# Gated heads over three gate groups, y chunk 7 last, half-width weights split early, x reloaded in portions: one layer of a hybrid encoder trunk on one core

## The reference

```
proj = h @ w_in              # ..., hog/gz (output gates of heads), gate_a, gate_b
o = rmsnorm(o_head, w) * silu(gate of the head)       # 4 HGRN2 heads, 4 delta heads
y_a = o_hg @ w_pa ;  y_b = o_gdn @ w_pb               # 512 -> 1024 each
y = sigmoid(gate_a) * y_a + sigmoid(gate_b) * y_b
x = x + g1 * (y @ w_out)
h = rmsnorm(x, norm_ffn) * (1 + sc2) + sh2
x = x + g2 * ((silu(h @ w_gate) * (h @ w_up)) @ w_down)
return rmsnorm(x, final_norm), new states
```

## Time and profile before

| | us |
|---|---|
| median of three runs | 1112.09 |
| the three runs | 1110.04, 1112.09, 3748.86 |
| the profiled execution, its own time | 1107.67 |
| its span, first to last instruction | 1105.1 |
| TensorE busy in the span | 1048.9 (95%) |
| VectorE, ScalarE busy | 486.3 (44%), 371.2 (34%) |
| mean granted TensorE clock | 0.983 |

### The profile page before, as it was taken

The page is one execution under the profiler, slowest core; times in us unless marked ns, Lnnn a source line. Parts: engine busy times, 40 slices in busy tenths (PEclk is TensorE's granted clock), DMA queues, the critical chain, the costliest instruction groups (busy, mean ns, idle before and its releaser), DMA issues.

```text
span 1105.1 us, 20527 instructions
## 1 busy us (share of the span) xinstructions
PE 1048.9 (95%) x8763; PEld 1009.7 (91%) x8763; DVE 486.3 (44%) x802; ACT 371.2 (34%) x635; POOL 58.0 (5%) x52
## 2 busy tenths in 40 slices
PE   6998999999999999998999997999999999999995
PEld 5887888889999999997999997999999999999995
DVE  3678535272224644735543366433323333233342
ACT  6665343513432234136223213322222222222122
POOL 0002220032201000000000000000000000000000
PEclk9999999999999999999999998999999999999997
DMA  9722222230323253332342322223233232222212
GB/s 328 223 58 58 58 77 58 59 110 21 96 77 112 77 136 108 98 94 78 123 131 70 113 77 77 72 81 95 76 95 88 82 90 82 86 87 89 80 43 81
DMA packets 181253, 103.42 MB, mean 94 GB/s; under 512 B 4498, under 2 KB 179032, under 8 KB 181180
## 3 DMA queue, kind: packets, MB, share of 16 engines
q1 hardware_dynamic: 179340, 96.28, 30.5%
q0 software_dynamic: 1216, 3.84, 1.0%
q10 hardware_dynamic: 624, 2.23, 0.6%
HBM read 99.02 MB, written 3.31 MB: 93 GB/s over the span
## 4 chain that ended last, share of the span: by engine, by line
PE 85%; DVE 6%; ACT 5%; issue 2%; DMA 1%; ACTq 0%; DVEq 0%
PE G L1584 67%; PE R L1590 14%; PE R L1593 2%; DVE cy L1510 1%; PE G L1624 1%; DVE w_lo L1164 1%; DMA raw<-in_w_in 1%; ACT w_hi L874 1%; ACT rn L902 1%; ACT sq L939 0%; ACT Um L911 0%; DVE relT L1341 0%; DMA xtok<-in_x_prompt 0%; ACT L851 0%; DVE val L1525 0%
## 5 line engine op out<-in xcount | busy, mean ns | idle before, releaser
L1584 PE MATMUL G<-h_hi,w_hi 128*128 128x272 f32 x1456 | 427.5, 294 | 10.4 <-DVE w_lo L1164 5.9
L1584 PE MATMUL G<-h_hi,w_lo 128*128 128x272 f32 x1456 | 423.0, 291 | 0.0
L1584 PE MATMUL G<-h_lo,w_hi 128*128 128x272 f32 x1456 | 420.7, 289 | 0.0
L1584 PEld LDWEIGHTS G<-h_hi,w_hi 128*128 128x128 f32 x1456 | 276.0, 190 | 13.1 <-issue 11.5
L1164 DVE TENSOR_TENSOR w_lo<-raw,w_hi 128x1024 fp32r<-128x1024 f32 (+2 forms) x139 | 166.6, 1199 | 261.5 <-ACT w_hi L874 261.0
L1584 PEld LDWEIGHTS G<-h_lo,w_hi 128*128 128x128 f32 x1456 | 276.4, 190 | 0.0
L1584 PEld LDWEIGHTS G<-h_hi,w_lo 128*128 128x128 f32 x1456 | 275.6, 189 | 0.0
L874 ACT ACTIVATE w_hi<-raw 128x1024 fp32r<-128x1024 f32 (+2 forms) x139 | 137.5, 989 | 122.9 <-PE G L1584 108.2
L1584 PE MATMUL G<-a_hi,w_hi 128*128 128x272 f32 x352 | 101.8, 289 | 0.0
L1584 PE MATMUL G<-a_hi,w_lo 128*128 128x272 f32 x352 | 101.7, 289 | 0.0
L1584 PE MATMUL G<-a_lo,w_hi 128*128 128x272 f32 x352 | 101.3, 288 | 0.0
(11 more groups left out here) (233 smaller groups left out, 1321.3 us busy)
## 6 DMA issues: line engine op xcount, KB each, us to landing
raw<-in_w_in SPq DMA_DIRECT2D x48, 512.0 KB, 5.7
raw<-in_w_up SPq DMA_DIRECT2D x44, 512.0 KB, 3.8
raw<-in_w_ada SPq DMA_DIRECT2D x32, 512.0 KB, 4.1
wada<-in_w_ada SPq DMA_DIRECT2D x8, 1024.0 KB, 10.9
raw<-in_w_down SPq DMA_DIRECT2D x16, 512.0 KB, 3.9
raw<-in_w_out SPq DMA_DIRECT2D x8, 512.0 KB, 4.0
raw<-in_w_down SPq DMA_DIRECT2D x8, 384.0 KB, 3.4
xtok<-in_x_prompt ACTq DMA_DIRECT2D x4, 512.0 KB, 5.6
```

The costliest lines, as they stand in the source:

```text
L1584: ins = pe.matmul(out, w, x, start=(job.first and k == 0 and p == 0), stop=(job.last and k == job.nk - 1 and p == 2))
```

## The change

Four edits. (1) The eight steps that gate the heads are spread over gate b3, gate a4 and gate b4: one between the halves of each of the three jobs, and two, two and one behind their evacuations; before, two stood ahead of gate b3 and none in or behind gate b4. (2) The weights of every pa m are split in steps of their own: ScalarE's part ahead of the last step that stands in the plan before pb m, VectorE's behind it. That last step is an ogate (m = 0), the bias step ada_mod 5 (m = 1), x_load (m = 2), the evacuation of pa m-1 (m = 3, 4) or of gate b m (m = 5 to 7). (3) In job out 0 the block k = 7 of both token halves is taken at the end, and VectorE makes the pending low part before it splits the next weights. (4) x comes back in four portions after pa 4, 5, 6 and 7, of two, two, two and three banks, in place of nine banks after pa 5.

```diff
--- before.py
+++ after.py
@@ -287,23 +287,25 @@
     weave(braid(hg_steps(1), norm_steps(range(2))),
           parts_of(*braid([gate(k, m) for m in range(EARLY - 1) for k in "ab"], ada_parts(4))))
     around(gate("a", EARLY - 1), norm_steps([2])[:1] + norm_steps([3])[:1], norm_steps([2])[1:] + norm_steps([3])[1:])
-    do("ogate", O_ORDER[0])
-    do("ogate", O_ORDER[1])
-    around(gate("b", EARLY - 1), [("ogate", n) for n in O_ORDER[2:4]], [("ogate", n) for n in O_ORDER[4:6]])
-    around(gate("a", EARLY), [("ogate", n) for n in O_ORDER[6:]], [])
-    gate("b", EARLY)()
+    for k, m, inside, after in (("b", EARLY - 1, O_ORDER[0:1], O_ORDER[1:3]), ("a", EARLY, O_ORDER[3:4], O_ORDER[4:6]),
+                                ("b", EARLY, O_ORDER[6:7], O_ORDER[7:8])):
+        around(gate(k, m), [("ogate", n) for n in inside], [("ogate", n) for n in after])
     for m in range(KD):
         if m > EARLY:
             gate("a", m)()
             gate("b", m)()
+        evac = plan.pop()
+        do("split_hi", len(jobs) + 1)
+        plan.append(evac)
+        do("split_lo", len(jobs) + 1)
         add("pb", m, [dict(w=tile(t["w_pb"], m * P), nk=NH, src="o", k0=NH)])
         add("pa", m, [dict(w=tile(t["w_pa"], m * P), nk=NH, src="o", k0=0)])
         if m == 0:
             do("ada_mod", 5)
         if m == 1:
             do("x_load")
-        if m == 5:
-            do("x_in")
+        if m >= EARLY:
+            do("x_in", m - EARLY)
     for m in range(KD):
         add("out", m, [dict(w=tile(t["w_out"], m * P), nk=KD, src="y", k0=0)])
     plan.insert(len(plan) - 1, ("split", len(jobs) + 1))
@@ -339,7 +341,7 @@
     n = len(FILLS)
     short = n if name not in ("g_x", "g_y", "g_t", "h_level") or a[1] < 5 else n - 1
     return {
-        "vectors": ["dve"] * 2, "x_first": ["act", "dve"] if name == "x_first" and a[0] < N_CHUNK else ["act"], "x_in": ["act"] * (KD + 1), "sums": ["act"] * 2, "onorm": ["act"] * 2,
+        "vectors": ["dve"] * 2, "x_first": ["act", "dve"] if name == "x_first" and a[0] < N_CHUNK else ["act"], "x_in": ["act"] * (3 if name == "x_in" and a[0] == KD - EARLY - 1 else 2), "sums": ["act"] * 2, "onorm": ["act"] * 2,
         "ada_rows": ["act"], "ada_T": ["dve"], "ada_mod": ["dve"] * 2, "g_rows": ["dve"], "g_norm": ["act"] * 2, "g_bcast": ["act"] * n, "g_gram": ["dve"] * (2 * n),
         "g_tok": ["act"] * n + ["dve"] * (2 * n),
         "g_x": ["dve" if name == "g_x" and a[1] == 0 else "act"] * short,
@@ -377,6 +379,7 @@
     duos = [s[1:] for s in plan if s[0] == "duo"]
     gab = duos[0][0]
     aside = {gab: "rec", duos[1][1]: "ffn"}
+    out0 = next(i for i, j in enumerate(jobs) if j.src == "y")
     early = [s[1] for s in plan if s[0] in ("split", "split_lo")]
     follows = dict(zip(split, split[1:]))
     ring = [i for i in split if i not in aside]
@@ -957,10 +960,12 @@
                     act.activation(c_cols[:, :, 0:2], vT[:, NA + VB["c"]:NA + VB["c"] + 2 * KD]
                                    .rearrange("p (g k) -> p k g", g=2), ACT.Silu).then_inc(c_sig, 1)
                 elif name == "x_in":
-                    wait_slot(act, groups_at["pa", EARLY - 1])
-                    read_banks(n, 0, [(xT[:, k, 0:SEQ], lambda b: R[:, b, 0:SEQ]) for k in range(KD)])
-                    read_banks(n, KD, [(xT[:, :, SEQ:TOK], lambda b: R[:, b, 0:KD * DEC]
-                                        .rearrange("p (k t) -> p k t", k=KD))])
+                    if a[0] == 0:
+                        wait_slot(act, groups_at["pa", EARLY - 1])
+                    read_banks(n, 0, [(xT[:, k, 0:SEQ], lambda b: R[:, b, 0:SEQ]) for k in (2 * a[0], 2 * a[0] + 1)])
+                    if a[0] == KD - EARLY - 1:
+                        read_banks(n, 2, [(xT[:, :, SEQ:TOK], lambda b: R[:, b, 0:KD * DEC]
+                                           .rearrange("p (k t) -> p k t", k=KD))])
                 elif name in ("sums", "onorm", "g_norm"):
                     rnorm(n, dict(sums=D, onorm=P, g_norm=1)[name])
                 elif name == "ada_rows":
@@ -1226,6 +1231,8 @@
                     seen["val"] += 2 * walk.passed
                     later[:] = [(v + 2 * walk.passed, k + 2 * walk.passed, *z) for v, k, *z in later]
                 if name in ("job", "duo"):
+                    if a[-1] == out0:
+                        low_parts()
                     if follows.get(a[-1]) not in (None, *early):
                         split_weights(follows[a[-1]])
                     low_parts()
@@ -1527,7 +1534,7 @@
                         wait_group(dve, g)
                         v = 2 if kind == "out" else 5
                         if kind == "out" and arg == 0:
-                            wait_bank(dve, last_bank[len(plan) - 1 - plan[::-1].index(("x_in",))])
+                            wait_bank(dve, last_bank[len(plan) - 1 - plan[::-1].index(("x_in", KD - EARLY - 1))])
                         for grp, half, inside, cols_ in PIECES:
                             ins = dve.scalar_tensor_tensor(xT[:, arg, cols_], G[:, s, half, inside],
                                                            mod[:, v * KD + arg, grp:grp + 1], xT[:, arg, cols_],
@@ -1626,9 +1633,13 @@
                         ins.then_inc(job_done, 1)
                     else:
                         pe.wait_ge(w_lo_done, walk.plus(nth_split[i] + 1, 4))
-                        products((i, 0))
+                        products((i, 0), ks=range(KD - 1) if i == out0 else None)
                 elif name == "half":
-                    products((a[0], 1))
+                    if a[0] == out0:
+                        products((a[0], 1), ks=range(KD - 1))
+                        products((a[0], 0), (a[0], 1), ks=(KD - 1,))
+                    else:
+                        products((a[0], 1))
                 elif name == "duo_part":
                     both = duos[0]
                     if a[0] == 0:
@@ -1657,11 +1668,13 @@
                                        x_diag[0:L, c, 0:L]) for j, k in enumerate(ks)])
                 elif name == "x_in":
                     pe.wait_ge(x_again, 32)
-                    for k in range(KD):
-                        fill(n, k, [tr(lambda b, c=c: R[:, b, c * P:(c + 1) * P], xtok[:, c, k * P:(k + 1) * P])
+                    for j in range(2):
+                        k = 2 * a[0] + j
+                        fill(n, j, [tr(lambda b, c=c: R[:, b, c * P:(c + 1) * P], xtok[:, c, k * P:(k + 1) * P])
                                     for c in range(N_CHUNK)])
-                    fill(n, KD, [tr(lambda b, k=k: R[:, b, k * DEC:(k + 1) * DEC],
-                                    xtok[0:DEC, N_CHUNK, k * P:(k + 1) * P]) for k in range(KD)])
+                    if a[0] == KD - EARLY - 1:
+                        fill(n, 2, [tr(lambda b, k=k: R[:, b, k * DEC:(k + 1) * DEC],
+                                       xtok[0:DEC, N_CHUNK, k * P:(k + 1) * P]) for k in range(KD)])
                 elif name == "ada_rows":
                     pe.wait_ge(c_sig, 1)
                     pe.wait_ge(ada_in[a[0]], 32)
```

## The result

The changed kernel takes 1097.93 us (median of four runs, 1095.65 to 1100.6) where before takes 1111.07 (the two ordinary runs of the section above and a third of 1108.86, with the long one). The long run still counts in this second median, so I don't use the difference of the medians. The ratio without it is 0.9898, 95% interval 0.9873 to 0.9922: 11.3 us less, between 8.7 and 14.1. That is under the 2% of the prediction's bound, and clear of noise.

What follows compares the result with a forecast made beforehand. TensorE, 85% of the chain, was taken as the bound, so only its idle time or clock could give gains. Terms 4.0 + 1.5 + 0.8 + 2.6 + 1.5 = 10.4 us gave 1097.3 or 1101.7; forecast 1100, range 1095 to 1107.

Steps and rivals of the forecast that it cites:

- the 2% of the prediction's bound: Whole time: 2% (22 us) is about what a measurement of this kernel can tell from no change.
- Part 1: Gates a4 and b4: TensorE's two waits on split weights go once heads are spread; gain 4.0 us.
- Part 2: Heads of pa 3 and pa 4: earlier splits remove both waits, the one at pa 2 stays; gain 1.5 us.
- Part 3: Transposes of x: portions remove a 1.1 us loss, three more changes of work cost about 0.1 each; net 0.8 us.
- Part 4: Out 0: taking y chunk 7 last removes TensorE's 2.46 us wait for the last low part; gain 2.6 us.
- the clock: Behind the out 0 wait, 630 to 635 us: the fall of the clock goes too; 1.5 us, bounds 0 or 1.5.
- its smallest margin: Gate b4: its split weights are ready with only 0.4 us to spare; margins elsewhere up to 1.1 us.
- The low end of my range: 1095 us: profiled time less 10.4 and less another 1.5 us clock fall drawn elsewhere by the gate waits, rounded down.
- The base: Whole time: 10.4 us off the profiled 1107.67 gives 1097.3, off the ordinary runs' median 1101.7; 1100 taken between.
- The transposes in portions: Portions of x: a rival case had every portion draw a clock fall, time 1101 to 1106; that rival's chance 0.13.
- The chain that gives part back: Rival at gate b4, the last head's low part and x banks: missed margins cut the gain to 6.8, 1104; chance 0.12.
- The load of x: Rival in front of gate a5: x arrives late, slower only if the load exceeds 27 us; 1113 at 30; chance 0.02.

Runs made afterwards that it cites:

- p2_splits: Kernel before with only the weights of pa m split ahead of the last step before pb m: pb 0 to out 0 takes 91.81 us, 1.66 less.
- p3_portions: Kernel before with only x coming back in four portions: pb 0 to out 0 takes 91.98 us, 1.5 less.
- before_again: Kernel before run once more with no edit: out 0 takes 8.96 us against 10.49, gate b3 to out 0's end 124.70.
- one_head_more: Changed kernel with one more head ahead of the split of gate b4's weights: 1.32 us wait at gate b4, gate b3 to pb 0 19.73 us.
- pa2_too: Changed kernel with ScalarE's split for pa 2 also ahead of the evacuation of pa 1: stretch 114.10 us, whole time 0.9901 of before, median 1097.45.
- x_after_gate: Kernel before with the nine banks of x in one go after gate a5 instead of pa 5: transposes 4.20 us, pb 0 to out 0 92.02 us.
- Part 1 alone: Kernel before with only the head gatings spread over gates b3, a4 and b4: stretch 122.55 us, 3.7 less; whole-time ratio 0.9992 over ten runs.

## Why the prediction was right, step by step

The forecast was 1100, the median is 1097.93, in the range. The mechanisms were right as well: every wait that was to go went, the one that was to stay at pa 2 stayed, and each part was tried alone. One term was mis-sized, and the base was partly luck. By its own terms:

| term | predicted us | measured us | where |
|---|---|---|---|
| Part 1, gates | 4.0 | 4.1 | 22.30 to 18.20, in two executions each |
| Part 2, pa 3 and pa 4 | 1.5 | 1.7 | p2_splits |
| Part 3, x | 0.8 | 1.5 | p3_portions, projections 93.47 to 91.98 |
| Part 4, the wait | 2.6 | 2.6 | before_again to changed |
| the clock | 1.5 | 1.5, four times in five | before against before_again |
| sum | 10.4 | 11.4 | the stretch, 126.26 to 114.86 |

*Part 1* held to a tenth, and its smallest margin too: 0.4 predicted, 0.3 found, and one_head_more shows that the margin is real. The `w_lo` of pa 0 is in time only with the early split of Part 2, as the replay had it: without Part 2 it comes late and costs 0.5 us.

*Part 2* held, the wait left at pa 2 included, because the step that the edit pops there is not the evacuation. pa2_too confirms that cause.

*Part 3* is the term that was mis-sized: 0.8 where 1.5 came, for two reasons of equal size. I took the loss from the printed wait of 1.00 us and made it 1.1. The true loss is the time of the whole group less what its transposes need when nothing holds them, 5.57 - 4.20 = 1.4 us (x_after_gate): 1.17 around the printed wait, and 0.21 that hid in four short waits for the next four banks, which the timeline doesn't print. And I took off 0.3 for three more changes of work, 0.1 each, from the one long matmul behind the transposes; they cost nothing. That makes 1.4; the last 0.1 is not explained.

*Part 4 and the clock.* The wait went as worked out (the last portion of x takes 1.57 us and not 1.3, which only adds to the cover). The fall was counted as if it always came; it came behind four of five such waits. The term is right in kind, and its expected size is some 1.2 (four fifths of 1.5). The low end of my range used a fall behind the waits of Part 1, which eight traces don't show.

*The base.* The profiled execution of before (1107.67) is shorter than all three of its ordinary runs; taking 1100 between the two bases could not be made much better from three runs, since one execution differs from another by up to 8 us in the part ahead of gate b3 (509.0 to 516.7 us in the traces of this case). That it came out within 2.1 us is partly luck: the terms were 1.0 short of the stretch, and the rest is the base. Nineteen later runs of before have a median of 1108.79 and eleven more 1109.04, which 10.4 less would make 1098.4 and 1098.6. The prediction also took 2% for about what a measurement can tell; four runs of a kernel told 1% clearly, with an interval half a per cent wide.

The transposes in portions drew no fall of the clock: 1.00 from 615 to 635 us in the changed kernel, as in the 5 us with the last sixteen of them here.

```profile
620.00:625.00 5.00, 5.00 (x45) 4.79 (x44) 2.70 (x4) 2.39 (x5) 0.00 (x0) 1.00 0.36 107
625.00:630.00 5.00, 5.00 (x42) 5.00 (x42) 2.39 (x5) 1.52 (x2) 0.00 (x0) 1.00 0.37 108
```

By the Trainium skill (page "TensorE: Matmul & The Clock Gate", section "Part 4: PE-mode transpose"), which has transposes not count as work in the way that matmuls do, a fall could have stood here; none does.

*The rivals.* The chain that gives part back is real only for Part 1 without Part 2. The load of x was never late: no wait for `xtok` is in any of the thirteen traces. What stays open is why the ten executions of Part 1 alone had the lower clock: the one trace of them has its falls ahead of gate b3, where no instruction is changed, behind the out 0 wait and behind out 0, so it may be chance, but no run shows that. Open too is what decides whether a wait of 2.5 us draws a fall, for which nothing was tried but repetition.

## What to carry to other kernels

Where engines follow one written list, the place of a weight split against other work on the same two engines decides whether TensorE waits: ahead of gatings and evacuations it cost nothing here, and one gating more ahead of it delayed it by 1.7 us. Replay the list with measured durations and write down each margin; a margin of 0.3 us held here, and one step too many turned into a wait of 1.32 us, a little over the 0.9 to 1.2 that the replay gave. Size a loss by the time of the group less the unhindered time of its instructions, not by the idle time that is printed, and compare stretches between two fixed instructions when the clock in an untouched part moves the whole time by more than the gain.

## What was unexpected in the hardware

The same wait of 2.46 us in the same kernel was followed by a fall to the lower clock (1.2 GHz) in one execution and by none in another, 1.5 us apart in the job that follows. Ahead of gate b3 the same instructions took from 509.0 to 516.7 us, and the start moved with the mean granted clock of the first 250 us, from 0.97 down to 0.94.
